# An encoder trunk in fp32 pairs: one output block finished by ScalarE and Pool, and three steps reordered in the output stages

## What is computed

```python
h = rms_norm(x, pre_g)
parts = _split(h @ w_in, WIDTHS)
...
mix = jnp.concatenate([oa.reshape(b, s, -1) * jax.nn.silu(ga),
                       ob.reshape(b, s, -1) * jax.nn.silu(gb)], axis=-1)
return x + rms_norm(mix @ w_out, post_g)
```

## Time and profile before

| | us |
|---|---|
| median of 3 runs | 1171.69 (1171.15 to 1172.39) |
| the profiled execution, its own time | 1171.55 |
| its span, first to last instruction | 1169.8 |
| TensorE busy | 1159.2 (99%) |
| VectorE busy | 738.8 (63%) |
| ScalarE busy | 590.1 (50%) |
| Pool busy | 101.1 (9%) |

### The profile page before, as it was taken

The page is one execution under the profiler, slowest core; times in us unless marked ns, Lnnn a source line. Parts: engine busy times, 40 slices in busy tenths (PEclk is TensorE's granted clock), DMA queues, the critical chain, the costliest instruction groups (busy, mean ns, idle before and its releaser), DMA issues.

```text
span 1169.8 us, 14599 instructions
## 1 busy us (share of the span) xinstructions
PE 1159.2 (99%) x5444; PEld 966.7 (83%) x5444; DVE 738.8 (63%) x847; ACT 590.1 (50%) x754; POOL 101.1 (9%) x148
## 2 busy tenths in 40 slices
PE   8999999999999999999999999999999999999997
PEld 6888888888888888888888888888888888888886
DVE  6676565666665965755665555565746567668654
ACT  6554454555656644565445444454444444446442
POOL 1000001000000300010100101102011002002100
PEclk9999999999999999999999999999999999999999
DMA  9866676744745875455667666676666666455741
GB/s 362 284 217 218 200 243 198 249 149 148 260 167 216 218 235 208 149 216 186 237 192 256 202 224 198 213 235 201 228 203 192 230 203 215 144 189 184 254 148 72
DMA packets 85815, 244.02 MB, mean 209 GB/s; under 512 B 33264, under 2 KB 50832, under 8 KB 60672
## 3 DMA queue, kind: packets, MB, share of 16 engines
q1 hardware_dynamic: 82416, 234.92, 59.9%
q0 software_dynamic: 2624, 7.75, 2.0%
q10 hardware_dynamic: 720, 0.61, 0.2%
HBM read 220.17 MB, written 8.39 MB: 195 GB/s over the span
## 4 chain that ended last, share of the span: by engine, by line
PE 95%; DVE 2%; ACT 1%; DMA 1%; issue 0%; ACTq 0%; DVEq 0%
PE acc L511 88%; PE bank_x L674 2%; PE bank_y L627 1%; DMA resid<-x_turned 1%; PE bank_x L658 1%; PE bank_x L670 1%; PE bank_y L616 1%; DVE w_lo L1093 1%; DVE mix L1358 1%; PE bank_y L623 0%; PE bank_y L643 0%; PE bank_x L643 0%; DVE probs L1349 0%; DVE resid L1413 0%; DVE mix_blocks L1369 0%
## 5 line engine op out<-in xcount | busy, mean ns | idle before, releaser
L511 PE MATMUL acc<-w_hi,act_hi 128*128 128x512 f32 x1560 | 615.5, 395 | 0.5 <-DVE w_lo L1093 0.2
L511 PE MATMUL acc<-w_lo,act_hi 128*128 128x512 f32 x1560 | 608.1, 390 | 0.0
L1093 DVE TENSOR_TENSOR w_lo<-raw,w_hi 128x2048 fp32r<-128x2048 f32 x192 | 442.3, 2307 | 177.8 <-ACT w_hi L783 177.6
L783 ACT ACTIVATE w_hi<-raw 128x2048 fp32r<-128x2048 f32 x192 | 367.9, 1916 | 292.6 <-PE acc L511 284.4
L511 PE MATMUL acc<-w_hi,act_lo 128*128 128x512 f32 x1560 | 417.6, 389 | 0.0
L511 PEld LDWEIGHTS acc<-w_hi,act_lo 128*128 128x128 f32 x1560 | 292.7, 188 | 62.2 <-DVE act_lo L1111 0.4
L511 PEld LDWEIGHTS acc<-w_hi,act_hi 128*128 128x128 f32 x1560 | 293.2, 188 | 59.1 <-issue 1.0
L511 PEld LDWEIGHTS acc<-w_lo,act_hi 128*128 128x128 f32 x1560 | 293.1, 188 | 57.2
L790 ACT ACTIVATE unit<-acc,pre_r 128x512 f32<-128x512 f32 x78 | 49.4, 685 | 123.9 <-PE acc L511 119.5
L447 POOL TENSOR_TENSOR rope_c<-unit,cst 128x256 f32<-128x256 f32 (+1 forms) x19 | 14.1, 742 | 747.0 <-ACT unit L790 596.4
L1258 DVE TENSOR_SCALAR mix<-bank_x 128x256 f32<-128x256 f32 (+1 forms) x24 | 10.1, 422 | 65.8 <-PE bank_x L674 65.8
(11 more groups left out here) (180 smaller groups left out, 600.4 us busy)
## 6 DMA issues: line engine op xcount, KB each, us to landing
raw<-weights SPq DMA_DIRECT2D x192, 1024.0 KB, 5.0
qk_raw<-postg SPq DMA_DIRECT2D x176, 64.0 KB, 2.0
p_moved<-p_blocks SPq DMA_DIRECT2D x16, 256.0 KB, 5.5
probs<-p_moved SPq DMA_DIRECT2D x64, 64.0 KB, 2.0
raw<-weights SPq DMA_DIRECT2D x7, 512.0 KB, 9.4
postg<-post_g POOLq DMA_DIRECT2D x2, 1024.0 KB, 8.1
resid<-x_perm POOLq DMA_DIRECT2D x2, 1024.0 KB, 8.8
p_moved<-p_blocks SPq DMA_DIRECT2D x16, 128.0 KB, 5.0
```

The lines of the kernel that those rows point to most:

```text
L511: m = nc.tensor.matmul(tiles[t][:, :], a[:, kt, t * P:(t + 1) * P], w[:, buf, kk * NB:(kk + 1) * NB], start=(kt == 0 and a is act_hi and w ...
L783: nc.scalar.activation(w_hi[:, at % SPLIT, :], raw[:, at % RAW, :], ACT.Copy).then_inc(S["hi_ready"], 1)
L1093: nc.vector.tensor_tensor(w_lo[:, at % SPLIT, :], raw[:, at % RAW, :], w_hi[:, at % SPLIT, :].bitcast(F32), ALU.subtract).then_inc(S["lo_r ...
```

## The change

There are three parts.

1. **The last tile's first block.** VectorE writes blocks 1, 2 and 3 of tile 1 only. ScalarE, after its root, waits for the reciprocal and for all scaled blocks and multiplies block 0 of `mix` by it in place; Pool waits for that (`last_scaled`) and adds the block to `resid`. SP sends tile 1's blocks in the order 1, 2, 3, 0 and waits for Pool (`last_added`) ahead of block 0.
2. **The turned blocks.** In slots 3 and 5 VectorE turns the blocks of `mix` behind the low part of chunk 5 or 7, as it did already in slot 1.
3. **The high part in slot 4.** ScalarE makes the high part of chunk 6 before it copies the accumulators out.

```diff
             for t in range(NT):
-                for n in range(OUT_BLOCKS):
+                for k, n in enumerate(((0, 1, 2, 3), (1, 2, 3, 0))[t]):
                     cols = slice(n * NB, (n + 1) * NB)
 
-                    sp.wait_ge(x_new[t], OUT_BLOCKS + n + 1)
+                    if (t, n) == (1, 0):
+                        sp.wait_ge(S["last_added"], 1)
+                    else:
+                        sp.wait_ge(x_new[t], OUT_BLOCKS + k + 1)
...
+            pool.wait_ge(S["last_scaled"], 1)
+            pool.tensor_tensor(resid[:, 1, 0:NB], mix[:, 1, 0:NB], resid[:, 1, 0:NB], ALU.add).then_inc(S["last_added"], 1)
...
                     if s == CHUNKS:
+                        split_hi(g0 + s + 2)
                         take(g0 + CHUNKS, 0, unit_out)
...
-                    if s < CHUNKS + len(OUT_ORDER):
+                    if s != CHUNKS:
                         split_hi(g0 + s + 2)
...
+            act.wait_ge(S["y_rdy"], 2 * NT)
+            act.wait_ge(S["y_scaled"], 2 * OUT_BLOCKS)
+            nc.scalar.activation(mix[:, 1, 0:NB], mix[:, 1, 0:NB], ACT.Copy, scale=post_r[:, 1:2]).then_inc(
+                S["last_scaled"], 1)
...
                         gate(layer, c)
-                        if c > 1:
-                            turn_mix_blocks(layer, c)
                     if s < CHUNKS + len(OUT_ORDER):
                         split_lo(g0 + s + 2)
-                    if s == GATE_SLOTS[1]:
+                    if s in GATE_SLOTS[1:]:
 
-                        turn_mix_blocks(layer, 1)
+                        turn_mix_blocks(layer, GATE_SLOTS.index(s))
...
-                new_x(layer, 1, (0, 1) if layer == 0 else range(OUT_BLOCKS))
+                new_x(layer, 1, (0, 1) if layer == 0 else range(1, OUT_BLOCKS))
```

More of the change, by code:

```diff
@@ L254, in build @@
                  "m_new m_diff m_exp m_wsum m_scaled "
-                 "pre_sq pre_sum pre_var pre_std pre_rdy other_zero lam_p lam_s lam_e bias_in bias_rdy "
+                 "pre_sq pre_sum pre_var pre_std pre_rdy other_zero last_scaled last_added lam_p lam_s lam_e bias_in bias_rdy "
                  "y_sq y_scaled y_sum y_var y_std y_rdy "
```

## The result

The changed kernel takes 1173.19 us (median of 17 runs, 1172.66 to 1175.38); the kernel before, run beside it, takes 1171.56 (17 runs, 1171.15 to 1172.66). The ratio is 1.0014, 95% interval [1.0008, 1.0021]: 1.6 us slower where the prediction said 0.2, and outside its range. The profiled execution takes 1173.1, its span is 1171.3, where before they were 1171.55 and 1169.8.

The account below looks back on a forecast made before the run. TensorE, busy 1159.2 us of a span of 1169.8, was taken as the bound. Layer 0's -0.83 and the end's +1.05 summed to +0.22, giving 1171.9 us from the median; range 1170.6 to 1172.8.

Parts of the forecast that it names:

- -0.83 for the turned blocks: Layer 0's output stage: low parts of chunks 5 and 7 come earlier, TensorE's two waits go, gaining 0.83 us.
- the slower chunk behind each wait: Layer 0: the chunk after each wait ran 0.12 to 0.13 slow; were that to stay, only -0.58 would be left.
- thinnest cover: Layer 0 before chunk 8: transposes go 2.22 later, yet VectorE is through at 413.66, chunk 8 begins at 414.28; cover 0.6 us.
- 0 for the high part in slot 4: Slot 4, both layers: making chunk 6's high part before the copies was to change nothing, 0 us.
- the meeting of Pool and VectorE: Tile 1's additions: Pool's gets in between VectorE's and holds VectorE for 1.13 us, so block 3 is done at 1167.62.
- the gap in the data: Tile 1's output: DMA share shows a gap between second and third block; data end at 1169.87 instead of 1168.82, +1.05.
- The question left open: Tile 1's additions: no row showed L1413's form, with its scalar, beside Pool; bounds of the term 0 and +1.05.
- The end: Tile 1's last additions and sends: output data were to end 1.05 us later, the last term of the sum.
- four rivals: Engines do not meet, 1170.9 (0.22); Pool behind all three, 1171.3 (0.1); late turned quarter, 1173.7 (0.07); layer 0 still held, 1172.7 (0.06).
- 1173.7: Rival, layer 0 before chunk 8: second turned quarter comes late, chunk 8 waits 1.8, sum +2.0; chance 0.07.
- 1172.7: Rival, layer 0: low part goes earlier but something else holds TensorE as long, only the end counts; chance 0.06.
- the 0.2% that the prediction set as the bound for a difference: Whole kernel: a measurement can tell about 0.2%, 2.3 us, from no change; within it 0.94, slower 0.04, faster 0.02.

Follow-up runs that it names:

- Experiment 6: Kernel before plus part 2 alone (turned blocks behind the low parts): 1170.7 us, ratio 0.9991 [0.9982, 1.0000].
- experiment 1: Kernel before plus parts 2 and 3, without part 1, so VectorE adds all four blocks of tile 1: 1170.7 us, ratio 0.9986 [0.9977, 0.9995].
- experiment 3: Kernel before plus parts 2 and 3, with ScalarE and Pool finishing block 0 of tile 0 instead of tile 1: 1171.34 us, ratio 0.9994 [0.9985, 1.0004].
- experiment 5: Changed kernel, but Pool's addition also waits for VectorE's three, so they never run together: 1173.87 us, ratio 1.0018 [1.0009, 1.0027].
- experiment 7: Kernel before plus parts 2 and 3 and a one-column Pool memset once tile 1's reciprocal is there: 1170.89 us, ratio 0.9992 [0.9983, 1.0001].

## Why the prediction missed

**Right: -0.83 for the turned blocks.** Chunks 3 to 8 take 27.20 instead of 28.03, exactly that, and the slower chunk behind each wait went with the wait. The transposes' transfers, the "thinnest cover", held for the reason given: SP's half stayed the later one and left 0.36 earlier. Experiment 6 shows that part 2 alone does it.

**Right: 0 for the high part in slot 4.** Experiments 1 and 6 have the same median.

**Right: the meeting of Pool and VectorE, and the gap in the data.** Pool was to hold VectorE for 1.13: block 3 took 1.75, some 1.0 more than its neighbours. Pool was to take clearly more than 1.3: it took 1.73, and 1.25 alone (estimate 1.30). The term was +1.05 and the data came 0.96 later. The question left open, whether L1413's form with its scalar behaves like an addition of two tensors, is answered: experiments 3 and 5 show it with and without the meeting. The Trainium skill, "SBUF — State Buffer", section "Who interferes with whom", has it that a VectorE instruction with two SBUF inputs contends with a Pool instruction that reads SBUF; the trace agrees, with 3.08 against 2.08 for the three.

**Wrong: "The end" as the last term of the sum.** It stopped at the last byte of the output and took the time from there to the span's end, 0.98, as fixed. But that time is set by whichever is later: SP, about a microsecond behind the data, or Pool's drain, which ends 4.81 to 4.83 behind Pool's last instruction, and 0.2 more. So "the program ends when the last has arrived", as it says of the end above, holds only while no engine closes later. The kernel before has no Pool instruction in its last 70 us, so the second never showed. With Pool's addition ending at 1166.24 the drain gives 1166.24 + 4.83 + 0.2 = 1171.3, the span as measured. Against the data's 1169.05 + 0.98 = 1170.03 that is the missing +1.27, and with it the sum becomes -0.83 + 1.05 + 1.27 = +1.5. Measured between the medians: +1.6.

The row that would have warned was there: line 144's drain of Pool, which in the kernel before ended 7.5 behind Pool's last DMA issue (1098.8 less 1091.3), beside VectorE's, which ended with its last addition. The prediction looked at what Pool's instruction would delay and not at what the program does behind an engine's last instruction. None of the four rivals had it. The two whose times come nearest to the measured one, 1173.7 and 1172.7, have TensorE held in layer 0, before chunk 8 or as before the change; with the chunks 5.44 apart neither came true, and their numbers are near by luck.

What stays open: what Pool does in these 4.8 us. The runs show only that it is the same behind a memset of one column and an addition of 512 columns, alone or beside VectorE. In all six runs Pool had been idle for 67 to 75 us before that instruction, and no run has a late computation by Pool without such a wait. One thing speaks against the idle time as the cause: behind DMA issues, after 6 to 7 us of idling, the drain also ended 5.1 behind the last issue (experiments 1 and 6; 7.5 in the kernel before).

**The better version.** Part 2 alone, or parts 2 and 3, takes 1170.7 (experiments 6 and 1), 1.1 to 1.2 below the kernel before and 2.5 below the changed one. Against the kernel before that is 0.1%, less than the 0.2% that the prediction set as the bound for a difference. The interval of experiment 1 excludes no change, that of experiment 6 just touches it, and those of experiments 3 and 7, which have parts 2 and 3 as well, include it.

## What to carry to other kernels

An engine that has been idle for a long time is not free at the end of a program: list the closing instructions of each engine, and how long each stands behind that engine's last work, before giving it some. Here Pool's last instruction has to end some 4 us before the last data of the output (4.83 + 0.2 - 0.98), or it sets the end, however small it is. And read the span's end as a race of several closes; the chain of waits shows only the work, and here it ended 4.5 us early.

## What was not expected of the hardware

- Pool's closing drain ends 4.81 to 4.83 us behind the end of its last instruction, in six runs, behind a memset of 0.10 and additions of 1.25 to 1.76 alike. VectorE's and ScalarE's end 0.05 or less behind theirs.
- A VectorE operation on 128 x 256 takes 0.40 from start to start where 128 x 512 takes 0.66 to 0.67, and a send of half a block landed only 0.1 sooner than one of a whole block.
